# One decoder layer on one core: the DMA queue asks for a chunk's weights before what the steps need, and a memory head's numerator is copied out of PSUM by ScalarE

## The reference, cut to what matters

```python
h = _rmsnorm(x, g_mix); z = h @ w_in + b_in
(aq, ak, av, af, mq, mk, mv, mi, mf, mo, cb, cc, cx, ga, gm, gc) = _split_cols(z)
ya = _fox_prompt(...)  or  _fox_sample(...)         # 8 heads x 64, forget gates; the sample reads 4 pages of K, V, log f a sequence
hm, c1, n1, m1 = _mlstm(mq, mk, mv, mi, m_logf, c0, n0, m0, chunk)   # 4 heads x 128
#   h_t = num / max(|den|, exp(-m_t)) for each head, then RMSNorm over the head, times sigmoid(mo)
yc = (cb * dwconv3(cc * cx)) @ w_oc
merged = sigmoid(ga) * (ya @ w_oa) + sigmoid(gm) * (ym @ w_om) + sigmoid(gc) * yc
x = x + merged @ w_o
x = x + (silu(dwconv3(h2 @ Wa) + b) * (h2 @ Wb)) @ w_down
x = x + sigmoid(_rmsnorm(x, g_ple) @ w_ple_gate) * (pe @ w_ple)
```

## Time and profile before

| | |
|---|---|
| median of 3 runs | 1675.43 us (1668.41 to 1676.34) |
| profiled execution | 1662.07 us, span 1660.3 us |
| PE busy | 1433.7 us (86%) |
| DVE, ACT, POOL busy | 603.3, 446.6, 490.7 us |
| HBM read, written | 109.72 MB, 7.35 MB |
| mean granted TensorE clock | 0.928 |

### The profile page before, as it was taken

One profiled execution on the slowest core, in us unless ns is written; L12 is line 12 of the kernel. 1 busy time (PEld: TensorE's weight loads), 2 busy tenths in 40 slices (PEclk: granted clock), 3 DMA queues, 4 the chain that ended last, 5 costly groups with the idle time before them and its releaser, 6 DMA issues.

```text
span 1660.3 us, 21709 instructions
## 1 busy us (share of the span) xinstructions
PE 1433.7 (86%) x9211; PEld 1255.5 (76%) x9211; DVE 603.3 (36%) x779; ACT 446.6 (27%) x738; POOL 490.7 (30%) x278
## 2 busy tenths in 40 slices
PE   4799999991987777988786969879999999999795
PEld 3798777671665455668675969869999999999794
DVE  2300222210000100032551642667773377155765
ACT  2233332430212212224333313123222222122331
POOL 2332433330211111112112322335343333333540
PEclk9899999996999888979988979989999999999897
DMA  5267432133354252224224463322232223222221
GB/s 126 25 86 113 53 43 40 31 34 86 108 90 107 64 89 77 34 36 39 39 32 94 84 90 71 101 64 65 78 89 79 88 79 87 81 86 71 70 64 62
DMA packets 198079, 118.49 MB, mean 71 GB/s; under 512 B 13377, under 2 KB 186697, under 8 KB 197820
## 3 DMA queue, kind: packets, MB, share of 16 engines
q1 hardware_dynamic: 194326, 115.81, 34.2%
q10 hardware_dynamic: 3656, 1.29, 0.3%
HBM read 109.72 MB, written 7.35 MB: 71 GB/s over the span
## 4 chain that ended last, share of the span: by engine, by line
PE 69%; DMA 10%; DVE 6%; ACT 5%; SPq 4%; issue 3%; POOL 2%; ACTq 1%; DVEq 0%
PE psum L1032 18%; PE psum L1033 17%; PE psum L1037 17%; DMA raw<-in_w_in 9%; PE psum L1189 2%; PE psum L1144 2%; SPq L457 1%; PE psum L1090 1%; PE psum L1092 1%; PE psum L1110 1%; DVE hn L1439 1%; POOL a_lo L594 1%; PE psum L1135 1%; SPq L477 1%; SPq L481 1%
## 5 line engine op out<-in xcount | busy, mean ns | idle before, releaser
L587 POOL TENSOR_TENSOR w_lo<-raw,w_hi 128x1024 fp32r<-128x1024 f32 (+3 forms) x180 | 393.8, 2189 | 1005.7 <-ACT w_hi L708 1005.5
L1032 PE MATMUL psum<-a_hi,w_hi 128*128 128x288 f32 x1760 | 499.9, 309 | 9.3 <-ACT gateM L713 7.3
L1033 PE MATMUL psum<-a_lo,w_hi 128*128 128x288 f32 x1760 | 485.1, 300 | 0.0
L1032 PEld LDWEIGHTS psum<-a_hi,w_hi 128*128 128x128 f32 x1760 | 341.5, 194 | 34.6 <-issue 25.3
L708 ACT ACTIVATE w_hi<-raw 128x1024 fp32r<-128x1024 f32 (+3 forms) x180 | 173.3, 964 | 637.5 <-PE psum L1037 331.5
L1033 PEld LDWEIGHTS psum<-a_lo,w_hi 128*128 128x128 f32 x1760 | 341.4, 194 | 2.8 <-issue 2.8
L1037 PE MATMUL psum<-a_hi,w_lo 128*128 128x288 f32 x1760 | 269.7, 295 | 0.0
L1037 PEld LDWEIGHTS psum<-a_hi,w_lo 128*128 128x128 f32 x1760 | 246.4, 188 | 0.1
L1032 PE MATMUL psum<-hid_hi,w_hi 128*128 128x288 f32 x352 | 95.3, 296 | 1.5 <-ACT w_hi L708 1.5
L1033 PE MATMUL psum<-hid_lo,w_hi 128*128 128x288 f32 x352 | 95.3, 295 | 0.0
L1678 DVE SCALAR_TENSOR_TENSOR y_f<-u_f,cols,y_f 128x512 f32<-128x512 f32 x44 | 74.2, 1686 | 1.6
(11 more groups left out here) (385 smaller groups left out, 1999.9 us busy)
## 6 DMA issues: line engine op xcount, KB each, us to landing
raw<-in_w_in SPq DMA_DIRECT2D x64, 512.0 KB, 8.4
raw<-in_w_up SPq DMA_DIRECT2D x44, 512.0 KB, 3.8
kp<-in_cache_k SPq DMA_DIRECT2D x32, 256.0 KB, 3.5
vp<-in_cache_v SPq DMA_DIRECT2D x32, 256.0 KB, 4.3
raw<-in_w_down SPq DMA_DIRECT2D x16, 512.0 KB, 4.0
xs<-in_x_prompt SPq DMA_DIRECT2D x8, 512.0 KB, 9.6
raw<-in_w_o SPq DMA_DIRECT2D x8, 512.0 KB, 4.1
raw<-in_w_ple_gate SPq DMA_DIRECT2D x8, 512.0 KB, 4.1
```

The source lines that it names most:

```text
L587: pool.tensor_tensor(w_lo[:, c % 3, 0:kt, :], raw[:, c % 3, 0:kt, :], w_hi[:, c % 2, 0:kt, :].bitcast(F32), ALU.subtract).then_inc(lo_read ...
L1032: pe.matmul(dst, w_hi[:, slot, k, :], xhi[:, at_tile[k], cols], start=(k == 0), stop=False)
L1033: pe.matmul(dst, w_hi[:, slot, k, :], xlo[:, at_tile[k], cols], start=False, stop=False)
```

## The change

SP's loop is turned round: `load(c)` comes first, and behind it what the steps of job c - 3 ask for. So that pages and states are not asked for too late, the steps at which `before` acts are lower: `past_rows_in` goes from step 36 to 33 and loses the first K pages, which become `first_keys` (step 35) and a request at step 38; the first V pages go from step 44 to 42, the later K pages from q % 8 = 2 and 4 to 1 and 3, the later V pages from q % 8 = 0 to 7 of the pair before, the C matrices from r = 21 to 20, their stores from r = 25 to 24. `tokens_out` keeps step 2. The semaphore of the C matrices is split in two, of four sequences each. `XT0` goes from 116 to 119.

In a memory head ACT copies the numerator out of bank 6 (`num_out`), DVE's second instruction on the denominator frees bank 7 (`den_out`), and the quotient is made in SBUF.

Besides, some semaphores are joined, `mixA` has one buffer, `gbias` is cleared by POOL, and the table `OFF` of SBUF offsets is a new one.

```diff
-XT0 = 116
+XT0 = 119
@@ past_rows_in
                         sp.dma_start(lpast[:, b, j, :], d["cache_logf"][...]).then_inc(lpast_in, 16)
+
+            def first_keys():
                 sp.wait_ge(qblk_ready, AH + 1)
                 sp.wait_ge(scores_done, 4 * AH)
-                for b2 in range(2):
-                    page_rows("cache_k", kp[b2], kp_in[b2], b2)
+                page_rows("cache_k", kp[0], kp_in[0], 0)
@@ before(step)
-                if step == 36:
+                if step == 33:
                     past_rows_in()
-                if step == SAMPLE0 + 3:
+                if step == 35:
+                    first_keys()
+                if step == 38:
+                    page_rows("cache_k", kp[1], kp_in[1], 1)
+                if step == SAMPLE0 + 1:
                     sp.wait_ge(pv_done, 4 * AH)
...
-                    if q % 8 == 2:
+                    if q % 8 == 1:
...
-                    if q % 8 == 4:
+                    if q % 8 == 3:
...
-                if q % 8 == 0 and 8 <= q < 32:
-                    p = q // 8
+                if q % 8 == 7 and 0 <= q < 24:
+                    p = q // 8 + 1
...
-                if r == 21:
+                if r == 20:
...
-                        sp.dma_start(c_st[:, b], ...).then_inc(c_in, 16)
+                        sp.dma_start(c_st[:, b], ...).then_inc(c_in[b // 4], 16)
...
-                if 25 <= r < 33:
-                    b = r - 25
+                if 24 <= r < 32:
+                    b = r - 24
...
-                if step == XT0 - 2:
+                if step == 112:
@@ SP's loop
             for c in range(NJ):
-                for step in STEP_OF.get(c - 2, ()):
+                load(c)
+                for step in STEP_OF.get(c - 3, ()):
                     before(step)
-                load(c)
@@ ACT, memory step r
+                h, rest = divmod(r - 10, 3)
+                if rest == 0 and 0 <= h < MH:
+                    act.wait_ge(mpv_done, 4 * (h + 1))
+                    act.activation(h_t[:, h, 0:TP], psum[:, 6, :], ACT.Copy).then_inc(num_out, 1)
@@ PE
-                        pe.wait_ge(h_ready, h)
+                        pe.wait_ge(num_out, h)
+                        pe.wait_ge(den_out, h)
@@ DVE, finish_head
-                link(dve.tensor_tensor(e, psum[:, 7, :], e, ALU.max))
+                dve.tensor_tensor(e, psum[:, 7, :], e, ALU.max).then_inc(den_out, 1)
+                dve.wait_ge(den_out, h + 1)
                 link(dve.reciprocal(e, e))
-                dve.tensor_tensor(h_t[:, h, 0:TP], psum[:, 6, :], e, ALU.mult).then_inc(h_ready, 1)
+                dve.wait_ge(num_out, h + 1)
+                link(dve.tensor_tensor(h_t[:, h, 0:TP], h_t[:, h, 0:TP], e, ALU.mult))
```

More of the change, by code:

```diff
@@ L148 @@
 OFF = {
[L149 to L163, removed]
@@ L164 @@
-    "y_t": 0, "y_rows": 29696,
+    "xs": 25600, "rows1": 22016, "rows2": 0, "ws": 50688, "ws_hi": 512, "ws_lo": 22528, "sq0": 46080, "hn0": 53760,
+    "xT0": 3584, "qk_a": 111904, "v_a": 22208, "v_p": 130336, "v_s": 19104, "kst": 1216, "gs": 62496, "lsg": 64800,
+    "ge": 3584, "ncum": 60192, "lf_tok": 1056, "nmax": 0, "rsum": 67104, "rinv": 22176, "ya_hi": 68384,
+    "ya_lo": 89888, "q_blk": 10912, "k_new": 21152, "probs": 77600, "pt": 1216, "cb": 5312, "cc": 32544, "cx": 23328,
+    "u_c": 41760, "c_rows": 11456, "c_last": 23040, "c_out": 2464, "gateC": 99104, "gateA": 6304, "mixA": 118816,
@@ new lines @@
+    "gateM": 23328, "mixM": 160, "merged": 41760, "kp0": 103712, "kp1": 113952, "vp": 124704, "kt_s": 5312,
+    "cums": 60192, "lrep": 111904, "lnew": 22208, "pts": 122144, "ls": 77600, "tmp64": 4512, "o_tok": 2464,
+    "lpast": 32, "qk_m": 23328, "qs_m": 137504, "v_m": 80672, "rows_m": 107296, "rs_t": 160, "m_p4": 60192,
+    "m_sm": 79648, "e_all": 99104, "vm_p": 129312, "k_p": 121120, "vm_s": 17056, "k_s": 77600, "e_ms": 16032,
+    "a_s": 15008, "w_s": 19200, "g_col": 19104, "wl_p": 22272, "wl_s": 22368, "n_t": 0, "a_last": 22336,
@@ new lines @@
+    "a_last_t": 128, "decay": 160, "h_t": 80672, "hs_s": 11680, "c_st": 60192, "c_t": 4512, "k_own": 6560,
+    "n0": 12960, "cp_st": 20224, "np_st": 10912, "qn": 2464, "num": 10656, "den": 3488, "sig_o": 89888,
+    "ym_hi": 30240, "mg_hi": 118816, "xs2": 60192, "xT": 4608, "sq": 89888, "hn": 72864, "f_rows": 94496,
+    "f_cols": 60192, "f_last": 55392, "hid_hi": 23040, "hid_lo": 112928, "u_f": 48384, "y_f": 0, "s_f": 46080,
+    "p_rows": 80672, "p_hi": 50784, "p_lo": 135968, "f_out": 61600, "gate_p": 0, "emb": 94496, "y_t": 23040,
@@ L165 @@
+    "y_rows": 41472,
 }
@@ L261, in build @@
         gateA = local("gateA", [P, 2, T])
-        mixA = local("mixA", [P, 2, T])
+        mixA = local("mixA", [P, T])
         gateM = local("gateM", [P, 3, T])
@@ L378, in build @@
         so_rows, sot_done = sem("so_rows"), sem("sot_done")
-        m0_in, mrow_ready, mb_done, mb_copied, em_done, em_ready, mside_done, mside_copied = (
-            sem(n) for n in ("m0_in", "mrow_ready", "mb_done", "mb_copied", "em_done", "em_ready", "mside_done", "mside_copied"))
+        mrow_ready, mb_done, mb_copied, em_done, em_ready, mside_done, mside_copied = (
+            sem(n) for n in ("mrow_ready", "mb_done", "mb_copied", "em_done", "em_ready", "mside_done", "mside_copied"))
         kscaled, qs_ready, mtok_done, mtok_copied, wl_sub, wl_ready = (
             sem(n) for n in ("kscaled", "qs_ready", "mtok_done", "mtok_copied", "wl_sub", "wl_ready"))
[L383 to L387, removed]
+        mqk_done, mdec_ready, mexp_done, mw_ready, mpv_done, num_out, den_out = (
+            sem(n) for n in ("mqk_done", "mdec_ready", "mexp_done", "mw_ready", "mpv_done", "num_out", "den_out"))
+        kw_ready, cp_done, cp_copied, n_in, nt_done, nt_copied, qn_ready, sqk_done, sdec_ready, sdexp_done, ssum_done = (
+            sem(n) for n in ("kw_ready", "cp_done", "cp_copied", "n_in", "nt_done", "nt_copied", "qn_ready", "sqk_done", "sdec_ready", "sdexp_done", "ssum_done"))
+        c_in, c_store = [sem(f"c_in{i}") for i in range(2)], sem("c_store")
         ctr_done, ctr_copied, inter_done, kown_ready, cadd_done, cnew_ready, n_new_ready = (
@@ L573, in _ @@
         def _(pool):
-            pool.memset(ws[:], 0.0).then_inc(ws_zero, 1)
+            pool.memset(ws[:], 0.0).then_inc(zeroed, 1)
+            pool.memset(gbias[:], 0.0).then_inc(zeroed, 1)
             pool.memset(ones[:], 1.0).then_inc(consts_ready, 1)
@@ L674, in _ @@
             act.dma_start(rows2[3 * FT:4 * FT, :], d["b_fconv"][0].rearrange("(t p) -> t p", p=P)).then_inc(rows_in, 16)
-            act.wait_ge(ws_zero, 1)
+            act.wait_ge(zeroed, 1)
             for r0, c0, n in ((0, COL_AF, 8), (32, COL_MI, 4), (64, COL_MF, 4)):
-                act.dma_start(ws[:, :, r0:r0 + n], w_in[:, :, c0:c0 + n]).then_inc(ws_in, 16)
-            act.wait_ge(gzero, 1)
+                act.dma_start(ws[:, :, r0:r0 + n], w_in[:, :, c0:c0 + n]).then_inc(gates_in, 16)
+            act.wait_ge(zeroed, 2)
             for r0, c0, n in ((0, COL_AF, 8), (32, COL_MI, 4), (64, COL_MF, 4)):
-                act.dma_start(gbias[r0:r0 + n, :], brows[c0:c0 + n].rearrange("(p o) -> p o", o=1)).then_inc(bias_in, 16)
-            act.dma_start(pages[0:1, :], d["page_table"].rearrange("b j -> (b j)").rearrange("(o n) -> o n", o=1)).then_inc(pages_in, 16)
-            act.dma_start(m0[:], d["state_mlstm_m"].rearrange("b l h -> h (l b)")).then_inc(m0_in, 16)
+                act.dma_start(gbias[r0:r0 + n, :], brows[c0:c0 + n].rearrange("(p o) -> p o", o=1)).then_inc(gates_in, 16)
+            act.dma_start(pages[0:1, :], d["page_table"].rearrange("b j -> (b j)").rearrange("(o n) -> o n", o=1)).then_inc(past_in, 16)
+            act.dma_start(m0[:], d["state_mlstm_m"].rearrange("b l h -> h (l b)")).then_inc(past_in, 16)
             for k in range(KD):
@@ L1414, in link @@
                 dve.wait_ge(dve_step, links[0])
-            dve.memset(gbias[:], 0.0).then_inc(gzero, 1)
             dve.wait_ge(cols_done, 1)
@@ L1698, in out_of @@
                     gate = {"oc": gateC[:, i % 2, :], "oa": gateA[:, i % 2, :], "om": gateM[:, i % 3, :]}[kind]
-                    dst = {"oc": merged[:, i, :], "oa": mixA[:, i % 2, :], "om": mixM[:]}[kind]
+                    dst = {"oc": merged[:, i, :], "oa": mixA[:], "om": mixM[:]}[kind]
                     dve.wait_ge(gemm_done, c + 1)
```

30 lines of the change are left out of this document (14 added, 16 removed).

## The result

The changed kernel takes 1581.45 us by the median of four runs (1578.16 to 1584.72), against 1671.92 (1662.10 to 1676.34) of the kernel before on the same chip: a ratio of 0.9466 with a 95% interval of 0.9415 to 0.9518. I had said 1586, range 1562 to 1618. In a later set on another occasion the same kernel took 1580.23 beside 1665.74 (0.9477, 0.9447 to 0.9506). The profiled execution took 1579.88 us, its span 1578.1. It is the span that is taken apart here, 82.2 us shorter than before. The medians lie further apart, 90.5 us in this set and 85.5 in the later one: the traced execution of before (1662.07) is the fastest of its four, and its executions spread over 14 us. These 3 to 8 us stand in no row of what follows.

The account below looks back on a forecast made before the run. SP's issue order was taken as the limit, not PE or the DMA engines. 5.5 + 46.5 + 15 - 10 + 12.3 + 11.9 + 1.5 = 82.7 us saved gave 1579.4 or 1592.7; forecast 1586, range 1562 to 1618.

Parts of the forecast that it names:

- Part 1: The 34.4 us gap before the copied-state sums: load 34 issued 4 us sooner and landing faster; 5.5 us saved.
- Part 2: Sample attention, 410 to 704 us: loads issued when their slot is free remove most gaps; 46.5 us saved.
- Rival A: Sample attention: a chain through three engines, hidden by late weights, keeps half of the gaps; 1613 us, chance 0.17.
- rival E: Loads stay late because SP still waits for banks, buffers or stores between them; 1642 us, chance 0.04.
- Rival D: Pages asked for too late behind loads, nine requests each late by 11 us; 1688 us, chance 0.03.
- Part 3: PE's clock rises as gaps go: 10 us saved in the sample attention, 5 in the heads and steps 96 to 98.
- Part 4: Start of the prompt's attention: token rows written behind load 16 make the K rows late for PE; 10 us lost.
- Rival B: Start of the prompt's attention: token rows delay K further, by slow packets or SP held back issuing; 1600 us, chance 0.12.
- Part 5: Memory's heads: PSUM banks freed earlier remove PE's three gaps of 4.1 us; 12.3 us saved.
- rival C: Memory's heads: the quotient from SBUF waits up to 2.4 us for POOL four times, delaying PE; 1596 us, chance 0.04.
- Part 6: Steps 96 to 98: load 70 goes earlier and shrinks a 13.0 us gap, C matrices still in time; 11.9 us saved.
- Part 7: The rest: XT0's transposing steps fill part of PE's 4.8 us wait for w_lo; 1.5 us saved, other edits nothing.

Follow-up runs that it names:

- e4: The changed kernel with SP's page-number reads and log f DMAs spread over steps 8 to 23, two of each a step: 1547.88 us (ratio 0.9282).
- e5: The changed kernel, weights still first, but every request of the steps at the step number it had before the change: 1597.31 us (ratio 0.9562).
- e2: The kernel before with the memory head's edit alone, the order of loads and requests unchanged: 1648.55 us (ratio 0.9873).
- e1: The changed kernel with the memory's head as it was before, so the new order alone: 1602.41 us (ratio 0.9605).
- e6: The changed kernel with the eight slow loads reading w_in's columns 128 further right: 1569.02 us (ratio 0.9386).
- e7: The changed kernel with the C matrices asked for ahead of load 71 instead of behind it: 1576.17 us (ratio 0.9451).
- e10: The changed kernel itself, unchanged, timed again in a later set beside the kernel before: 1580.23 us (ratio 0.9477).
- e8: The changed kernel with page-number reads and log f DMAs spread, C matrices ahead of load 71, token rows ahead of load 16: 1532.24 us (ratio 0.9197).

## Why the prediction held, point by point

*Part 1* was right in place and 2 us too large (3.2 for 5.5). Load 34 was issued at 411.96, 35.6 us after job 30's end against 39.7 before, as I had it; but it landed after 10.8 us and not 8.4. With e4, which moves nothing but SP's block, the whole gap goes: the block was its cause.

*Part 2* was right: 44.6 us of gaps against 46.5. L1153 has none, L1188 one of 3.5 (I had said 2 to 3), and ACT's wait is 60.0 where I had said under 60. But only 35.5 of it is part 1's, where I had said nearly all, and in part 2 I had expected no late chunk that holds ACT: for five more chunks ACT still waits 3.2 to 7.0 us. They cost PE little: its idle time in the whole window is 4.6 us. Rival A, a second cause, and rival E are excluded by the window: 4.6 us of idle time are left in 212. Rival D did not occur in after, and e5 shows how far off it was: pages up to a job later added nothing from job 40 to 67.

*Part 3* was right in kind and too small: 15.3 where I had 10, and in the heads 6.4 where I had half of 5. My bound went by the stretch's mean clock, and I took a value near its lower end, on the thought that the clock falls only some way into a gap of 4 to 8 us. What the short gaps cost in addition was a third of their length in the sample attention (15.3 of 44.6) and half in the heads (6.4 of 11.6). Other traces bear both out: PE's busy time from job 34 to 51 is 212.6 and 213.4 us in before and e2, which have these gaps, and 197 to 200 in the nine others that lack them (e5, with its own gap, has 200.4); in the heads it is 72.8 and 73.0 with the gaps (before, e1) and 64 to 66 without. It is not so for a long gap: the 31.3 us of part 1 cost 1.7 more than their length (e4).

*Part 4* was right in its place and 2.7 too small. The step that was off is how the K rows become late: I had SP issue them at once and the queue drain them behind load 16. In the trace SP itself needed 12.7 us to issue them. Of load 16's slow place, on which my sum rested, e6 shows the share: with other columns the rows are issued in 10.6 us, and PE's gap is 6.0 and not 10.7. So some 5 us of it are the slow load, and most of the rest is that the rows begin 16 us later than before, counted from the end of job 12. Rival B named SP's issuing, as held back behind load 16, for 14 us more; a fifth of that came.

*Part 5* was right: the gaps are gone, to 0.3 us, and the copies on ACT cost nothing. The rule on the shared SBUF read was not put to the test by the quotient: now from SBUF alone, it took 0.69 us in all four heads (691 to 692 ns), exactly as from PSUM before. The Trainium skill (SBUF — State Buffer, "Who interferes with whom") tells of a wait for a GpSimd instruction that reads SBUF at the same moment; no such meeting fell on these four, for the nearest w_lo is 2.4 us away. Where one does, in the same stretch of after, the trace agrees: a product of 128x128 with both inputs in SBUF, which takes 0.29 alone, ends just behind POOL's w_lo (DVE, then POOL):

```profile
747.07 1.31 DVE L1562 TENSOR_TENSOR decay<-decay,cst 128x128 f32<-128x128 f32 x1
```

```profile
746.97 1.27 POOL L593 TENSOR_TENSOR w_lo<-raw,w_hi 128x512 fp32r<-128x512 f32 x1 [2.30 <-ACT w_hi L714]
```

So the wait on which rival C rests exists in this kernel. The quotient happens to miss it, and PE no longer waits for the quotient.

*Part 6* was right for the gap (13.0 to 1.1) and wrong for the C matrices, for which I had a microsecond to spare: they came 2.8 us late. I had given them their landing but not their issue. For all eight it took 11.6 us behind load 71; for the first four, which are those that PE waits for, 7.6 where e7 has 2.0. With e7's order the part gives 14.2, and I had said 14.4 with the clock.

*Part 7* named the gap for w_lo, and it fell from 4.8 to 3.3 us, the 1.5 that I had said. The stretch around it, from job 79 to 88, gives 2.3 in these two traces, but 60.2 to 60.9 us in most other kernels with the new XT0 and 60.5 and 62.0 with the old one: in time the part cannot be told from nothing.

The closeness of the sum (82.7 and 82.2) is in part luck: by the table, the sample attention, the heads, part 7 and the places elsewhere gave 9.2 us more than I said, and the parts 1, 4 and 6 gave 9.7 less. So is that of the time. The sum gave 1579.4 from the traced execution and 1592.7 from the median, and I took the middle; measured was 1581.45, because the saving between medians was larger than the one between the traces.

## What to carry to other kernels

Where one queue issues both a steady stream and requests that wait for buffers, let the stream go first whenever its slot is free, and look where each request stands in terms of issue time, not of landing alone. A block of scalar reads and small DMAs ahead of a load made a gap at both places at which it was tried (31.3 and 41.1 us); moving it moved the gap, spreading it removed it. And gaps on TensorE cost more than their length: here a third to a half more for gaps of 3 to 8 us, and a twentieth more for one of 31.

## What the runs showed that I had not expected

- SP's issue time depends on what is ahead in its queue. Eight C DMAs took 4.9 us of SP ahead of a load and 11.6 behind one; four DMAs of K pages, 7.0 us behind load 34, where eight of them had taken 3.95 before. What in the queue makes SP wait was not tried.
- Loads that cover the columns 576 to 640 above a multiple of 1024 of this matrix (rows of 32832 bytes) take 12.3 to 13.6 us alone in the queue where others take 5.6 to 8.6. This was measured for this matrix at its place in memory alone; whether the row length or the address makes it was not tried.
- The stretch from job 51 to 59 has the same gaps (8.7 to 8.9 us) and the same work in all kernels, and takes either 84.6 to 86.1 us (before, after, e10 and six others) or 77.8 to 79.2 (e1, e7, e8). In after and e7 PE's busy time there is 76.8 and 69.8 us at a granted clock of 0.82 and 0.89. So some 6 us between two single traces can be nothing but this, and I read e7 by its own stretch for that reason.
